# Two-layer hybrid blocks on one core: in blocks of 256 tokens, eight 512-column matmuls and then eight 256-column ones, in place of alternating pairs

## Chip, cores and metric

The kernel runs on one core of one Trainium2 chip. The time is device microseconds (us) of one execution on that core. Of the kernel before, three executions are timed; their median stands for it. A profile is of one execution.

## What is computed

The reference runs two transformer-like models, one behind the other, on a sequence of 256 tokens of width 1024 (16 meta tokens are set ahead of them for the first model). Each model has two layers, and each layer is a mixer and a squared-ReLU MLP, both added to a residual stream after an RMS norm. All data are fp32:

```python
def first_block(...):
    for layer in range(DEPTH):
        hn = rms_norm(h, g_mix[layer])
        if layer % 2 == 0:
            h = h + attention_mixer(hn, ...)
        else:
            h = h + short_conv_mixer(hn, w_in_conv[j], conv_w[j], w_out_conv[j])
        h = h + sq_relu_mlp(rms_norm(h, g_mlp[layer]), w_mlp_up[layer], w_mlp_down[layer])

def sq_relu_mlp(h, w_up, w_down):                  # w_up 1024 x 4096, w_down 4096 x 1024
    return jnp.square(jax.nn.relu(h @ w_up)) @ w_down
```

The second model has a differential attention and an mLSTM mixer, each again with an MLP of width 4096. So the order of the work is: attention (stage names a_...), MLP 0 (up0, dn0), convolution (c_in, c_out), MLP 1 (up1, dn1), differential attention (d_in, d_out), MLP 2 (up2, dn2), mLSTM (m_in, m_out), MLP 3 (up3, dn3). Up to the convolution the kernel carries 272 or 258 tokens, since the meta tokens and the convolution's halo are needed; from the last third of c_in on it carries the 256 tokens of the output only.

## The kernel before

Every weight matrix is cut into blocks of 1024 inputs by 128 outputs (one "feature block"). Weights come from HBM by DMA into four `raw` buffers of two blocks each. For each block, ScalarE writes the high part `whi` (rounded to the format that TensorE multiplies fast, fp32r) at line 545, and VectorE the remainder `wlo` = raw - whi at line 1113. Both sit in a ring of four buffers. Activations are kept as such a pair too: `x2`, `y2` and `hid2` hold for each slice of 128 inputs the high part of all tokens and then the low part. In the profile they are named x, y and hid.

A block's product is the sum over eight slices k of whi·xhi + whi·xlo + wlo·xhi. TensorE (the program `pe`) does it in one of two ways:

- `product` (lines 1973 to 1975): three matmuls a slice, each over all tokens (272, 258 or 256 columns), into the same PSUM columns.
- `paired` (lines 1979 and 1980), for 256 tokens: one matmul of 512 columns, whi against xhi and xlo side by side, fills both halves of a PSUM bank, and one matmul of 256 columns adds wlo·xhi to the second half. VectorE adds the halves when it reads the bank (line 1132).

`linear` (line 1998) does one block: `free_bank` waits until the bank has been read, then comes a wait for `w_lo` (both weight parts are there), the eight slices, and with the last matmul an increment of `w_used`, which gives the ring buffer back to ScalarE. Where `ready` is given (block 0 of a stage), TensorE also waits for each slice of the activations by itself. In `mlp` the up projection is a loop of four passes over eight blocks, through `linear`; block 0 of every pass has `ready`. The down projection is a loop of two passes over 16 blocks, and four consecutive blocks with the same output accumulate in one bank; `hid_ready` is waited for ahead of each. `d_out` and `m_out` call `paired` themselves, with blocks interleaved, and the second input projections `d_in` and `m_in` use `product`. MLP 3's down projection (`out_block`, lines 2558 to 2560) is laid out the other way round: activations are stationary, the weights stream through as 512 columns, three matmuls a slice, all of 512 columns.

Each engine's program is written out by hand, in order; engines are bound to each other by semaphores alone. Every matmul is preceded by its own load of 128x128 weights (LDWEIGHTS, PEld in the profile).

Of the kernel before, what the change touches and what calls it, by code (L numbers as in the profile page):

```python
# [12 lines left out]
KB = D // P  # L13
# [4 lines left out]
FB = FF // P  # L18
# [18 lines left out]
S = SEQ  # L37
# [9 lines left out]
RING = 4  # L47
# [97 lines left out]
def build(nc, d, out):  # L145
# [5 lines left out]
    for b, (_, g, _) in enumerate(blocks):  # L151
        last_block[g] = b
# [20 lines left out]
    with ExitStack() as ctx:  # L173
# [4 lines left out]
        def sb(name, shape, dt=F32, at=ctx):  # L178
            return at.enter_context(nc.sbuf_tensor(name, shape, dt))
# [4 lines left out]
        PS = ctx.enter_context(nc.psum_tensor("PS", [P, 8, 512], F32))  # L184

        raw = [sb(f"raw{i}", [P, 2 * D]) for i in range(RAW)]
        whi = [sb(f"whi{i}", [P, D], F32R) for i in range(RING)]
        wlo = [sb(f"wlo{i}", [P, D], F32R) for i in range(RING)]
# [17 lines left out]
        with ExitStack() as s:  # L206
            hid2 = sb("hid2", [P, FB * 2 * (T - HALO)], F32R, s)
            hh, hl = (hid2, 0), (hid2, 1)
# [60 lines left out]
        w_hi, w_lo, w_used, psum_read = Z["w_hi"], Z["w_lo"], Z["w_used"], Z["psum_read"]  # L269
# [4 lines left out]
        def std(ap):  # L274
            return ap.rearrange("p (k c) -> p k c", k=KB)
# [37 lines left out]
        def at(buf, n, tok):  # L313

            if isinstance(buf, tuple):
                return buf[0][:, bass.ds(n * (2 * T) + (buf[1] + tok[0]), tok[1])]
            return buf[:, bass.ds(n * T + tok[0], tok[1])]

        def hid(buf, n, count):
            return buf[0][:, bass.ds(n * (2 * count) + buf[1] * count, count)]  # L320

        def both(buf, k, tok):

            return buf[0].rearrange("p (k a t) -> p k a t", k=KB, a=2)[:, k, :, tok[0]:tok[0] + tok[1]]

        def both_hid(n, count):
            return hid2[:, n * 2 * count:(n + 1) * 2 * count].rearrange("p (a t) -> p a t", a=2)
# [33 lines left out]
        def bank(stage, o):  # L361

            if stage == "d_in":
                return D_T_BANK if o == 3 else o % 3
            return (O[stage] + o + 1) % PSR

        def a_bank(o):

            if o in (4, 5):
                return o + 2  # L370
            return (o + 1) % PSR if o < A_LEAD or o >= O["a_om"] else (o + 1) % 2
# [1595 lines left out]
        def _(pe):  # L1967
            mm = nc.tensor.matmul

            def product(b, k, cols, xs_hi, xs_lo, dst, first, last):  # L1970

                whi_b, wlo_b = cols(whi[b % RING], k), cols(wlo[b % RING], k)
                mm(dst, whi_b, xs_hi, start=first, stop=False)  # L1973
                mm(dst, whi_b, xs_lo, start=False, stop=False)  # L1974
                return mm(dst, wlo_b, xs_hi, start=False, stop=last)  # L1975

            def paired(b, k, xs_hi, xs_both, dst, first, last):

                mm(dst.rearrange("p (a t) -> p a t", a=2), std_cols(whi[b % RING], k), xs_both, start=first, stop=False)  # L1979
                return mm(dst[:, S:2 * S], std_cols(wlo[b % RING], k), xs_hi, start=False, stop=last)  # L1980

            def std_cols(buf, k):
                return std(buf[:, :])[:, k, :]

            def free_bank(stage, o, i=0):

                back = 3 if stage == "d_in" and o != 3 or stage == "d_out" and o < 3 else PSR
                if stage == "m_in" and o >= PSR:
                    j = o - PSR
                    if j in V_LAST or j + 1 in V_LAST:  # L1990
                        hd = (V_LAST.index(j) if j in V_LAST else V_LAST.index(j + 1))
                        pe.wait_ge(Z["m_vread"], TS * hd + 1 + (j in V_LAST))
                    else:
                        pe.wait_ge(psum_read, m_reads(j))
                elif O[stage] + o >= back:
                    pe.wait_ge(psum_read, i + (O[stage] + o - back + 1))

            def linear(stage, j, xhi, xlo, tok, ready=None, i=0, o=None, pair=False):


                b = B[stage] + j
                o = j if o is None else o
                free_bank(stage, o, i)
                pe.wait_ge(w_lo, i + (b + 1))
                order = [k for k, _ in ready[1]] if ready else range(KB)
                for n, k in enumerate(order):
                    if ready:
                        pe.wait_ge(ready[0], ready[1][n][1])
                    if pair:
                        last = paired(b, k, at(xhi, k, tok), both(xhi, k, tok), PS[:, bank(stage, o), :], n == 0, n == KB - 1)  # L2010
                    else:
                        last = product(b, k, std_cols, at(xhi, k, tok), at(xlo, k, tok), PS[:, bank(stage, o), 0:tok[1]],
                                       n == 0, n == KB - 1)
                last.then_inc(w_used, 1)

            def linear_first(stage, xhi, xlo, tok, ready, i=0, late=1):

                order = ready[1]
                for some in (order[:-late], order[-late:]):
                    for j in range(2):  # L2020
                        b = B[stage] + j
                        if some[0] is order[0]:
                            free_bank(stage, j, i)
                            pe.wait_ge(w_lo, i + (b + 1))
                        for k, count in some:
                            if j == 0:
                                pe.wait_ge(ready[0], count)
                            last = product(b, k, std_cols, at(xhi, k, tok), at(xlo, k, tok), PS[:, bank(stage, j), 0:tok[1]],
                                           k == order[0][0], k == order[-1][0])
                        if some[-1] is order[-1]:  # L2030
                            last.then_inc(w_used, 1)

            def x_blocks(n):

                return Z["x_ready"], [(k, 8 * n + k + 1) for k in range(KB)]
# [21 lines left out]
            def mlp(m, tok):  # L2057
                up, dn = f"up{m}", f"dn{m}"
                with pe.Fori(0, FB // 8) as i:
                    if m == 0:  # L2060
                        linear_first(up, xh, xl, tok, x_blocks(1), i * 8, 2)
                    for j in range(0 if m else 2, 8):
                        linear(up, j, xh, xl, tok, x_blocks(2 * m + 1) if j == 0 else None, i * 8, pair=m > 0)
                norm(2 * m + 1, tok[1])
                if m == 3:
                    return
                with pe.Fori(0, 2) as i:
                    for j in range(16):
                        ng, kc, n = j // 8, j % 8 // 2, j % 2
                        o, b = 2 * ng + n, B[dn] + j  # L2070
                        if kc == 0:
                            free_bank(dn, o, i * 4)
                        pe.wait_ge(w_lo, i * 16 + (b + 1))
                        pe.wait_ge(Z["hid_ready"], 2 + FB * m + KB * (kc + 1))
                        for k in range(KB):
                            kk = kc * KB + k
                            if m:
                                last = paired(b, k, hid(hh, kk, S), both_hid(kk, S), PS[:, bank(dn, o), :], kk == 0, kk == FB - 1)
                            else:
                                last = product(b, k, std_cols, hid(hh, kk, tok[1]), hid(hl, kk, tok[1]),  # L2080
                                               PS[:, bank(dn, o), 0:tok[1]], kk == 0, kk == FB - 1)
                        last.then_inc(w_used, 1)
# [3 lines left out]
            for _ in range(WARM):  # L2086
                last = mm(PS[:, 7, 0:2 * P], wlo[RING - 1][:, 0:P], wlo[RING - 1][:, 0:2 * P], start=True, stop=True)
# [140 lines left out]
            for some in (range(KB // 2), range(KB // 2, KB)):  # L2228
                for j in range(2):
                    pe.wait_ge(w_lo if some[0] else Z["w_first_lo"], j + 1)  # L2230
                    for k in some:
                        if j == 0:
                            pe.wait_ge(Z["x_ready"], k + 1)
                        last = product(B["a_in"] + j, k, std_cols, at(xh, k, FULL), at(xl, k, FULL), PS[:, a_bank(j), 0:T],
                                       k == 0, k == KB - 1)
# [16 lines left out]
            for n in range(N_A + 2):  # L2252
# [24 lines left out]
                m = n - 13  # L2277
# [239 lines left out]
            for j in range(2, M_BLOCKS):  # L2517
# [6 lines left out]
                if j == ROW_AT[0]:  # L2524
                    pe.wait_ge(Z["mg_rows"], 1)
                    pe.wait_ge(Z["m_rtok"], 1)
                    for a in range(TS):
                        last = nc.tensor.transpose(PS[:, MISC, a * ML_HEADS:(a + 1) * ML_HEADS], mgate[:, 5, a * P:(a + 1) * P],
                                                   ident[0:ML_HEADS, 0:ML_HEADS])
# [33 lines left out]
            for c in range(2):  # L2563
                whole = 16 if c == 0 else 16 - RING
                for j in range(whole):
                    for a in range(TS):
                        last = out_block(c, j, a)
                    last.then_inc(w_used, 1)
                    if c == 0 and j == 4:
                        pe.wait_ge(w_lo, B["dn3"] + RING + 1)  # L2570
                        pe.wait_ge(Z["norm_read"], 8)
                        for a in range(TS):
                            last = mm(PS[:, MISC, a:a + 1], rstd2[0:1, a * P:(a + 1) * P], ident[0:1, 0:1], start=True, stop=True)
                        last.then_inc(Z["out_rt"], 1)
            for a in range(TS):
                for j in range(16 - RING, 16):
                    last = out_block(1, j, a)
# [47 lines left out]
```

## Time and profile before

| | |
|---|---|
| median of 3 executions | 1220.39 us (1219.93 to 1220.52) |
| profiled execution, first to last instruction | 1219.5 us |
| TensorE busy | 1206.3 us, 99%, 8112 matmuls |
| VectorE busy | 900.6 us, 74% |
| ScalarE busy | 715.2 us, 59% |
| GpSimd busy | 251.7 us, 21% |
| HBM read | 206.69 MB, 172 GB/s over the span |

The profile gives no time for the profiled execution other than its span; the median of the timed ones lies 0.9 us above it. Busy times of TensorE count overlapping instructions once. A matmul's record runs from its start to its modelled end, some 150 ns past the start of the next one. So what a matmul costs is read from start to start (here called its step), not from the duration of its record.

### The profile page before, as it was taken

The numbers are of one execution on the slowest core, as the hardware profiler recorded it, in microseconds if no ns is written. First come the engines' busy times: TensorE is split into PE (matmuls) and PEld (weight loads), VectorE is DVE, ScalarE is ACT, GpSimd is POOL, SyncE is SP. The second block draws the span as 40 slices with busy tenths as digits, with TensorE's granted clock in tenths as the row PEclk, the third lists the DMA queues.
The fourth block names the chain that finished last, engine by engine and source line by source line (L and its number), as shares of the span: only waits on it lengthen the run. The fifth ranks groups of instructions, "written<-read, shape, count | busy, mean of one in ns | idle before, by whom it ended". The sixth has DMA issues, their size and how long they took to land.

```text
span 1219.5 us, 23664 instructions
## 1 busy us (share of the span) xinstructions
PE 1206.3 (99%) x8112; PEld 1105.9 (91%) x8112; DVE 900.6 (74%) x1554; ACT 715.2 (59%) x1306; POOL 251.7 (21%) x260
## 2 busy tenths in 40 slices
PE   8999999999999999999999999999999999999997
PEld 8998999999999988888899998888889998888886
DVE  5788877565557988775669868786667988877764
ACT  5657656564444556664447876665445787666343
POOL 4000024220010114430020003442102811444000
PEclk9999999999999999999999999999999999999999
DMA  9214236655557556555656427665555645665550
GB/s 295 93 44 152 79 108 205 186 191 175 178 194 231 174 173 207 183 195 174 199 182 203 140 86 212 185 190 189 173 173 174 207 139 149 215 194 183 186 193 35
DMA packets 194693, 208.79 MB, mean 171 GB/s; under 512 B 6103, under 2 KB 183352, under 8 KB 194488
## 3 DMA queue, kind: packets, MB, share of 16 engines
q1 hardware_dynamic: 192256, 202.78, 52.1%
q10 hardware_dynamic: 2360, 5.00, 1.3%
q8 instruction: 45, 0.74, 0.3%
q14 instruction: 32, 0.26, 0.1%
HBM read 206.69 MB, written 2.64 MB: 172 GB/s over the span
## 4 chain that ended last, share of the span: by engine, by line
PE 88%; DVE 5%; ACT 4%; issue 2%; DMA 0%; ACTq 0%; DVEq 0%
PE PS L1979 28%; PE PS L1980 14%; PE PS L1973 10%; PE PS L1974 10%; PE PS L1975 10%; PE PS L2558 2%; PE PS L2559 2%; PE PS L2560 2%; PE PS L2191 1%; PE PS L2213 1%; PE PS L2147 1%; DVE wlo L1113 1%; ACT whi L545 1%; PE PS L2322 1%; PE PS L2320 1%
## 5 line engine op out<-in xcount | busy, mean ns | idle before, releaser
L1113 DVE TENSOR_TENSOR wlo<-raw,whi 128x1024 fp32r<-128x1024 f32 x368 | 453.1, 1238 | 161.6 <-ACT whi L545 158.7
L545 ACT ACTIVATE whi<-raw 128x1024 fp32r<-128x1024 f32 x368 | 386.5, 1053 | 310.9 <-PE PS L1980 168.9
L1979 PE MATMUL PS<-x,whi 128*128 128x512 f32 x832 | 291.8, 395 | 0.2
L1980 PE MATMUL PS<-x,wlo 128*128 128x256 f32 x832 | 234.4, 282 | 0.0
L1973 PE MATMUL PS<-x,whi 128*128 128x258 f32 (+2 forms) x800 | 231.7, 290 | 0.8 <-issue 0.8
L1974 PE MATMUL PS<-x,whi 128*128 128x258 f32 (+2 forms) x800 | 229.0, 286 | 0.0
L1975 PE MATMUL PS<-x,wlo 128*128 128x258 f32 (+2 forms) x800 | 227.2, 284 | 0.0
L1979 PEld LDWEIGHTS PS<-x,whi 128*128 128x128 f32 x832 | 156.3, 188 | 36.5 <-DVE x L1090 1.2
L1882 POOL TENSOR_TENSOR act_s<-act_r 128x256 f32<-128x256 f32 (+1 forms) x128 | 143.5, 1121 | 211.0 <-ACT act_r L607 150.1
L1979 PE MATMUL PS<-hid,whi 128*128 128x512 f32 x512 | 179.0, 395 | 0.2
L1862 POOL TENSOR_TENSOR acc<-acc,sq 128x256 f32<-128x256 f32 (+2 forms) x64 | 54.0, 844 | 584.0 <-ACT sq L589 234.9
L1980 PEld LDWEIGHTS PS<-x,wlo 128*128 128x128 f32 x832 | 157.2, 189 | 0.0
L1973 PEld LDWEIGHTS PS<-x,whi 128*128 128x128 f32 x800 | 152.3, 190 | 2.7 <-issue 1.9
L1974 PEld LDWEIGHTS PS<-x,whi 128*128 128x128 f32 x800 | 151.3, 189 | 0.4
L1975 PEld LDWEIGHTS PS<-x,wlo 128*128 128x128 f32 x800 | 151.5, 189 | 0.0
L1980 PE MATMUL PS<-hid,wlo 128*128 128x256 f32 x512 | 142.6, 279 | 0.0
L1979 PEld LDWEIGHTS PS<-hid,whi 128*128 128x128 f32 x512 | 96.0, 187 | 23.1 <-DVE wlo L1113 0.8
L1132 DVE TENSOR_REDUCE tmp<-PS 128x256 f32<-128x512 f32 x120 | 82.8, 690 | 43.0 <-PE PS L1980 41.3
L1980 PEld LDWEIGHTS PS<-hid,wlo 128*128 128x128 f32 x512 | 96.4, 188 | 0.1
L1974 PE MATMUL PS<-hid,whi 128*128 128x258 f32 x256 | 72.6, 284 | 0.0
L1973 PE MATMUL PS<-hid,whi 128*128 128x258 f32 x256 | 72.4, 283 | 0.0
L1975 PE MATMUL PS<-hid,wlo 128*128 128x258 f32 x256 | 71.9, 281 | 0.0
(317 smaller groups left out, 2013.4 us busy)
## 6 DMA issues: line engine op xcount, KB each, us to landing
raw<-in_mlp_w SPq DMA_DIRECT2D x64, 1024.0 KB, 5.4
raw<-in_w_mlp_up SPq DMA_DIRECT2D x32, 1024.0 KB, 5.5
raw<-in_w_mlp_down SPq DMA_DIRECT2D x32, 1024.0 KB, 5.0
raw<-in_w_in_conv SPq DMA_DIRECT2D x12, 1024.0 KB, 5.0
raw<-in_attn_w_in SPq DMA_DIRECT2D x12, 1024.0 KB, 5.1
raw<-in_mlstm_w_in SPq DMA_DIRECT2D x12, 1024.0 KB, 5.8
raw<-in_w_in_attn SPq DMA_DIRECT2D x8, 1024.0 KB, 8.0
raw<-in_w_out_attn SPq DMA_DIRECT2D x4, 1024.0 KB, 5.0
```

The costliest lines, as they stand in the source:

```text
L545: A(part_view(whi, b), raw_view(b), ACT.Copy).then_inc(w_hi, 1)
L1113: V.tensor_tensor(part_view(wlo, b), raw_view(b), f32(part_view(whi, b)), ALU.subtract).then_inc(w_lo, 1)
L1132: return V.tensor_reduce(o, PS[:, bk, :].rearrange("p (a t) -> p t a", a=2), mybir.AxisListType.X, ALU.add)
L1862: Gp.tensor_tensor(acc[:, 0:count], acc[:, 0:count], sq[:, k % 2, 0:count], ALU.add).then_inc(Z["acc_ready"], 1)
L1882: Gp.tensor_tensor(act_s[:, j % 2, 0:count], act_r[:, j % 2, 0:count], act_r[:, j % 2, 0:count], ALU.mult)\
L1973: mm(dst, whi_b, xs_hi, start=first, stop=False)
L1974: mm(dst, whi_b, xs_lo, start=False, stop=False)
L1975: return mm(dst, wlo_b, xs_hi, start=False, stop=last)
L1979: mm(dst.rearrange("p (a t) -> p a t", a=2), std_cols(whi[b % RING], k), xs_both, start=first, stop=False)
L1980: return mm(dst[:, S:2 * S], std_cols(wlo[b % RING], k), xs_hi, start=False, stop=last)
L2558: mm(dst, x_h, w_h, start=k == 0, stop=False)
L2559: mm(dst, x_h, w_l, start=False, stop=False)
```

## The change

A new helper, `paired_block`, does a whole block: first the eight 512-column matmuls with `whi`, slice after slice, then the eight 256-column ones with `wlo`. `linear` uses it where `pair` holds and no `ready` is given, and `mlp` uses it in the down projections of MLP 1 and 2. Block 0 of every pass or stage that has `ready`, `d_out`, `m_out`, all of `product`, and `out_block` stay as they were. The number of matmuls, their sizes, their operands, the waits ahead of a block and the increment behind it are the same. In the new file the lines are 1985 (512 columns) and 1987 (256 columns).

```diff
+            def paired_block(b, xs_hi, xs_both, dst, first, last):
+
+                for k in range(KB):
+                    mm(dst.rearrange("p (a t) -> p a t", a=2), std_cols(whi[b % RING], k), xs_both(k), start=first and k == 0, stop=False)
+                for k in range(KB):
+                    done = mm(dst[:, S:2 * S], std_cols(wlo[b % RING], k), xs_hi(k), start=False, stop=last and k == KB - 1)
+                return done
+
...
                 free_bank(stage, o, i)
                 pe.wait_ge(w_lo, i + (b + 1))
+                if pair and not ready:
+                    last = paired_block(b, lambda k: at(xhi, k, tok), lambda k: both(xhi, k, tok), PS[:, bank(stage, o), :], True, True)
+                    last.then_inc(w_used, 1)
+                    return
...
                         pe.wait_ge(Z["hid_ready"], 2 + FB * m + KB * (kc + 1))
-                        for k in range(KB):
+                        if m:
+                            k0 = kc * KB
+                            last = paired_block(b, lambda k: hid(hh, k0 + k, S), lambda k: both_hid(k0 + k, S), PS[:, bank(dn, o), :],
+                                                kc == 0, kc == FB // KB - 1)
+                        for k in range(0 if m else KB):
                             kk = kc * KB + k
-                            if m:
-                                last = paired(b, k, hid(hh, kk, S), both_hid(kk, S), PS[:, bank(dn, o), :], kk == 0, kk == FB - 1)
-                            else:
+                            if not m:
```

On TensorE, where the last third of c_in begins (behind the last 258-column block), the order before reads as follows; the last two rows go on alternating until 16 matmuls are done:

```order
L1974 MATMUL PS<-x,whi 128x258
L1975 MATMUL PS<-x,wlo 128x258
L1979 MATMUL PS<-x,whi 128x512 [waits w_lo,psum_read]
L1980 MATMUL PS<-x,wlo 128x256
L1979 MATMUL PS<-x,whi 128x512
```

The same place in the changed kernel, the first two blocks of the 256-token part:

```order
L1974 MATMUL PS<-x,whi 128x258
L1975 MATMUL PS<-x,wlo 128x258
L1985 MATMUL PS<-x,whi 128x512 [waits w_lo,psum_read]
L1985 MATMUL PS<-x,whi 128x512 x7
L1987 MATMUL PS<-x,wlo 128x256 x8
L1985 MATMUL PS<-x,whi 128x512 [waits w_lo,psum_read]
```

Seven 256-column matmuls moved behind seven 512-column ones; the wait of a block is still with its first matmul. On TensorE at the start of a down projection (MLP 1), before:

```order
L2067 UNCONDITIONAL_BRANCH
L2067 ISA
L2073 ISA [waits psum_read]
L1979 MATMUL PS<-hid,whi 128x512 [waits hid_ready,w_lo]
L1980 MATMUL PS<-hid,wlo 128x256
L1979 MATMUL PS<-hid,whi 128x512
```

and in the changed kernel:

```order
L2079 UNCONDITIONAL_BRANCH
L2079 ISA
L2085 ISA [waits psum_read]
L1985 MATMUL PS<-hid,whi 128x512 [waits hid_ready,w_lo]
L1985 MATMUL PS<-hid,whi 128x512 x7
L1987 MATMUL PS<-hid,wlo 128x256 x8
```

The loop's branch and the waits stand where they stood. The programs of VectorE, ScalarE and SyncE are the same, instruction for instruction, and GpSimd's differs only in line numbers.

## Rows read from the trace of the kernel before

**Rows 1.** The page: busy time, TensorE's clock by slice (9 is full), the chain's shares.

```profile
PE 1206.3 (99%) x8112; PEld 1105.9 (91%) x8112; DVE 900.6 (74%) x1554; ACT 715.2 (59%) x1306; POOL 251.7 (21%) x260
...
PEclk9999999999999999999999999999999999999999
...
PE 88%; DVE 5%; ACT 4%; issue 2%; DMA 0%; ACTq 0%; DVEq 0%
```

**Rows 2.** What TensorE waited for: us in total, times, longest; the two longest.

```profile
PE PS L2147 <- ACT asq L696: 2.6, 1, 2.6
PE PS L2087 <- DVE wlo L1257: 1.5, 1, 1.5
```

**Rows 3.** Groups by form: busy us, mean ns of one record, idle us before.

```profile
L1979 PE MATMUL PS<-x,whi 128*128 128x512 f32 x832 | 291.8, 395 | 0.2
...
L1979 PE MATMUL PS<-hid,whi 128*128 128x512 f32 x512 | 179.0, 395 | 0.2
L1980 PE MATMUL PS<-hid,wlo 128*128 128x256 f32 x512 | 142.6, 279 | 0.0
...
L1979 PE MATMUL PS<-y,whi 128*128 128x512 f32 x192 | 68.6, 400 | 0.1
```

**Rows 4.** Timeline of TensorE in up1: start us, us of the record, then the instruction.

```profile
467.80 0.39 PE L1979 MATMUL PS<-x,whi 128*128 128x512 f32 x1
468.03 0.28 PE L1980 MATMUL PS<-x,wlo 128*128 128x256 f32 x1
468.15 0.40 PE L1979 MATMUL PS<-x,whi 128*128 128x512 f32 x1
...
473.40 0.39 PE L1979 MATMUL PS<-x,whi 128*128 128x512 f32 x1
```

**Rows 5.** Timeline in dn1, first pass (two rows) and second pass (two rows).

```profile
545.20 0.39 PE L1979 MATMUL PS<-hid,whi 128*128 128x512 f32 x1
...
587.84 0.40 PE L1979 MATMUL PS<-hid,whi 128*128 128x512 f32 x1
...
610.37 0.40 PE L1979 MATMUL PS<-hid,whi 128*128 128x512 f32 x1
...
615.66 0.40 PE L1979 MATMUL PS<-hid,whi 128*128 128x512 f32 x1
```

**Rows 6.** Timeline in dn3 (512 columns only): two stretches behind an interruption.

```profile
1125.34 0.39 PE L2559 MATMUL PS<-wlo,hid 128*128 128x512 f32 x1
...
1127.19 0.39 PE L2558 MATMUL PS<-whi,hid 128*128 128x512 f32 x1
...
1139.71 0.40 PE L2559 MATMUL PS<-wlo,hid 128*128 128x512 f32 x1
...
1141.55 0.39 PE L2558 MATMUL PS<-whi,hid 128*128 128x512 f32 x1
```

**Rows 7.** One line of dn3: records, ns min/median/max, first and last start us.

```profile
L2558 PE MATMUL PS<-whi,hid x96: 389/389/389, 1144.9 to 1209.5; 128*128 128x512 f32 x96
```

**Rows 8.** Timeline in m_in (256 columns only), two blocks.

```profile
939.20 0.28 PE L2456 MATMUL PS<-whi,x 128*128 128x256 f32 x1
...
943.86 0.28 PE L2457 MATMUL PS<-wlo,x 128*128 128x256 f32 x1
...
949.77 0.28 PE L1973 MATMUL PS<-x,whi 128*128 128x256 f32 x1
...
952.62 0.28 PE L1973 MATMUL PS<-x,whi 128*128 128x256 f32 x1
```

**Rows 9.** Timeline in d_in: six matmuls of 128 columns merged.

```profile
717.66 0.83 PE L2373 MATMUL PS<-d_pT,dvt 128*128 128x128 f32 x6
```

**Rows 10.** Stretch of up1: us, then busy us of each engine (instructions), clock, DMA.

```profile
455.00:540.00 85.00, 85.00 (x488) 74.62 (x487) 70.52 (x103) 55.01 (x92) 37.26 (x30) 1.00 0.60 187
```

## Prediction

> **What bounds the kernel now.** I read the page first: TensorE is busy 99% of the span, at the full clock (2.4 GHz) in every slice, and the chain that ended last lies on it for 88% [rows 1]. The view of its waits says the same from the other side: the two longest together are 4.1 us, both in the first attention, far from the change [rows 2]. In the groups by form the two lines that the change touches show 0.2 us of idle time [rows 3]. So a nanosecond taken out of each matmul there goes to the end, and what matters is the step, the time from one start to the next. The busy view can't give it, since records overlap; the timeline can.
>
> In up1, line 1979 starts at 467.80 us, line 1980 at 468.03 and 1979 again at 468.15; 16 pairs later it is 473.40 [rows 4]. So the 512-column matmul takes a step of about 231 ns, the 256-column one about 118 or 119, and a pair (473.40 - 467.80) / 16 = 350.0 ns. The columns alone need 512 / 2.4 + 256 / 2.4 = 320 ns at the granted clock, so 30 ns a pair are overhead. That overhead isn't one number. In the first pass of dn1, 123 pairs (16 blocks less five pairs) take 587.84 - 545.20 = 42.64 us, 346.7 ns each; in the second pass, 15 pairs take 615.66 - 610.37 = 5.29 us, 353 ns each [rows 5]. Same line, same operands, same clock, different loop pass: TensorE falls into a rhythm and stays in it, and rhythms differ by some 3 ns a pair.
>
> **What the change touches.** Blocks done by the new helper: 8 of c_in, 7 of c_out, 7 of 8 in each of 4 passes of up1, up2 and up3 (84), and 32 in each of dn1 and dn2 (64). That is 163 blocks, 1304 of the 1536 pairs that line 1979 shows [rows 3]. Before, I take 350.0 ns for the 99 blocks of x and y, 346.7 for three of the four down passes and 353 for the fourth (dn2's passes are both taken like dn1's first), which gives (99 x 350.0 + 48 x 346.7 + 16 x 353) / 163 = 349.3 ns a pair.
>
> **What is only moved.** Waits stay with the first matmul of a block and the increment of `w_used` with the last, so ScalarE, VectorE and SyncE see the same events, each earlier or later only by what TensorE gains or loses. Nothing is queued differently on their queues or on the DMA queues. A block takes 8 x 350 = 2.80 us. VectorE is busy 70.5 of 85.0 us in up1, ScalarE 55.0 [rows 10], so TensorE may take 1% less time there and their work still hides; VectorE would become the bound only if TensorE took 17% less. The blocks with per-slice waits keep the old order. All of this I cost at nothing.
>
> **The 512-column matmuls.** Seven of eight in a block are now followed by another of 512 columns, and no row shows that for x or hid as the moving operand. The nearest is dn3, where all are of 512 columns and the weights move. Settled, a triple there takes (1209.5 - 1144.9) / 95 = 680 ns, so the step is 226.7 ns [rows 7], some 4 ns less than in a pair. But it isn't so at once: behind an interruption eight steps take 1127.19 - 1125.34 = 1.85 us (231 ns each) in one place and 1141.55 - 1139.71 = 1.84 us (230 ns) in another [rows 6]. In the changed kernel a run is only eight long, and the 256-column run between two of them is a small interruption. The cost lies between 226.7 (settled) and 231 (never settles). I take 229, the middle.
>
> **The 256-column matmuls.** These now follow each other as in the `product` blocks of 256 tokens. There 40 steps take 943.86 - 939.20 = 4.66 us, 116.5 ns, in one place, and 24 steps take 952.62 - 949.77 = 2.85 us, 118.8 ns, in another [rows 8]. I take 118, close to what one has in a pair now. A load of weights must hide under one such step, where before every second load had a 512-column matmul to hide under. That looks like a new risk, but six matmuls of 128 columns, each with its own load, take 0.83 us with the last one's record in it [rows 9]; less that record (about 0.28) they step by 0.55 / 5 = 110 ns. A load thus needs at most 110 ns and fits under 118, as it does in the rows of m_in.
>
> **The sum.** A pair goes from 349.3 to 229 + 118 = 347.0 ns: -2.3 ns x 1304 = -3.0 us. The span goes from 1219.5 to 1216.5 us. The timed median lies 0.9 us above the span, so I predict 1217.4 us. The bounds of the two unknowns give 226.7 + 116.5 = 343.2 ns a pair (-8.0 us) and 231 + 118.8 = 349.8 ns (+0.7 us).
>
> A rule weighed against this. The rows show that the step is not the columns over the clock plus a constant: 230 to 231 and 226.7 ns for the same 512 columns [rows 4, 7]. The Trainium skill, in "TensorE: Matmul & The Clock Gate", section "Back-to-back issue gap", gives a warm gap of N / 2.4 + 2.5 ns, whoever the neighbour is. By it the sum would be zero, as the order doesn't enter, and its own size (215.8 ns) is under every step of 512 columns above. It is the second rival below.
>
> **The rivals.**
>
> 1. Full settling. The runs of 512 columns reach the settled step within a matmul or two. For it: dn3 holds 226.7 for 64 us on end [rows 7]. Against it: it took longer than that behind both interruptions [rows 6]. A pair at 226.7 + 116.5 to 118: -8.0 to -6.0 us, so about 1213.5 us.
>
> 2. No difference. The order doesn't matter: 231 ns belong to any 512-column matmul that has x or hid moving, and dn3 is quick because its operands are laid out differently. Then a pair stays at 349 to 350 ns, and the time is 1220.4 us, within 1 us. For it: both interrupted stretches show 231 and 230 [rows 6], which is the step of the pairs, and nothing in the trace shows a settled 512-column step with x moving. Against it: the interrupted stretches did settle in the end, with the same operands. (This is where the skill's formula leads; the trace disagrees with its size, and can't yet say about the order.) To this case belongs the one in which TensorE is faster but some stage's end hangs on another engine; rows 10 leave little room for that.
>
> 3. A worse rhythm: slower. The second pass of dn1 shows that the same instructions can lock into 353 ns a pair for a whole pass [rows 5]. The new order is a new rhythm of 16 matmuls, and it may lock into such a one in all stages. The price is 353 - 349.3 = 3.7 ns x 1304 = +4.8 us, so 1225.2 us. It decides the sign from 349.3 ns a pair on, and can be measured from 351.2 ns (2.44 us / 1304 = 1.9 ns above). For it: one of four down passes is in it. Against it: three of four are not, nor any of the up stages I looked at, and the runs of equal length in rows 6 to 8 all lie at or under the steps of the pairs.
>
> **How the numbers follow.** A measurement of this kernel can tell about 0.2%, 2.44 us, from no change. My forecast (some 347 ns a pair, 1215.5 to 1219.5 us) gets 0.43, full settling 0.12, no difference 0.32, the worse rhythm 0.13. A part of the forecast's case, 0.07, lies above 1217.95 and would count as the same. So faster is 0.36 + 0.12 = 0.48, the same 0.32 + 0.07 = 0.39, slower 0.13. The range leaves out about a third of full settling at the low end and half of the worse rhythm at the high end: 1213.4 to 1223.0 us.
>
> **What would show it.** In the timeline of up1 after, eight rows of line 1985 in a row: their steps should be above 226.7 at first and fall towards it, with a mean near 229; eight rows of line 1987 at 116 to 119. Block to block should be 8 x 347 = 2.776 us instead of 2.800. `d_out`, `m_out`, dn3 and the `product` blocks should keep their steps, and the waits of TensorE should stay where they are. The prediction is wrong in kind if the 512-column steps inside a run stay at 231 (second rival), if they exceed 234 or the 256-column ones exceed 120 (third), or if steps fall as forecast but a wait for `wlo` or for a bank grows on TensorE in the up stages.

## Result and the profile after

The change makes the kernel slower by about a quarter of a per cent. Nine executions of each give 1223.67 us after (1223.42 to 1224.37) and 1221.10 us before (1219.93 to 1221.35); the ratio is 1.0024, with a 95% interval of 1.0014 to 1.0033. The forecast was 1217.4 us with a range of 1213.4 to 1223.0. The time lies outside it, on the slow side, 1.5 us short of the third rival's 1225.2 us.

| | before | after |
|---|---|---|
| median of nine | 1221.10 us | 1223.67 us |
| profiled span | 1219.5 us | 1221.7 us |
| TensorE busy | 1206.3 us | 1207.8 us |
| a pair in up1 to up3, inside a pass | 350.0 ns | 354.2 ns in most blocks, 352.9 over a pass |
| a pair in dn1 | 346.7 ns, then 353.4 ns | 349.2 ns |
| a pair in dn2 | 346.7 ns | 349.2 ns |

First the page of the kernel after, for what did not move; it answers to [rows 1]:

```profile
PE 1207.8 (99%) x8112; PEld 1106.1 (91%) x8112; DVE 899.8 (74%) x1554; ACT 715.0 (59%) x1306; POOL 251.4 (21%) x260
...
PEclk9999999999999999999999999999999999999999
...
PE 89%; DVE 5%; ACT 4%; issue 2%; DMA 0%; ACTq 0%; DVEq 0%
```

TensorE is still busy 99% at the full clock, and the other engines do the same work. Its waits, with those of before in [rows 2] (lines are numbered anew):

```profile
PE PS L2161 <- ACT asq L696: 2.6, 1, 2.6
PE PS L1973 <- issue: 1.6, 1, 1.6
PE PS L2101 <- DVE wlo L1257: 1.5, 1, 1.5
```

The 1.6 us ahead of L1973 stand 9.7 us into the execution, far ahead of the change; the kernel before has 0.8 us at the same line. No wait came with the change, and the groups of the two new lines show none (us idle before them in the last column), as [rows 3] did:

```profile
L1985 PE MATMUL PS<-x,whi 128*128 128x512 f32 x736 | 188.4, 398 | 0.0
L1985 PE MATMUL PS<-hid,whi 128*128 128x512 f32 x512 | 128.8, 393 | 0.1
L1987 PE MATMUL PS<-x,wlo 128*128 128x256 f32 x736 | 102.0, 281 | 0.0
```

So the loss is in the steps themselves. The timeline of TensorE merges equal neighbours; one block of up1 and the start of the next read:

```profile
468.41 2.05 PE L1985 MATMUL PS<-x,whi 128*128 128x512 f32 x8
470.30 1.11 PE L1987 MATMUL PS<-x,wlo 128*128 128x256 f32 x8
471.25 0.40 PE L1985 MATMUL PS<-x,whi 128*128 128x512 f32 x1
```

Eight steps of 512 columns take 470.30 - 468.41 = 1.89 us, 236 ns each, and eight of 256 columns 0.95 us, 119 ns each. In the alternating order of up1 the 512-column steps are 231 and 234 ns by turns, 232.4 on average, and the 256-column ones 117.6. So the 512-column step is some 4 ns worse than before, and 10 ns worse than the settled step of [rows 7]. A block of dn1:

```profile
547.85 2.00 PE L1985 MATMUL PS<-hid,whi 128*128 128x512 f32 x8
549.69 1.11 PE L1987 MATMUL PS<-hid,wlo 128*128 128x256 f32 x8
550.64 0.40 PE L1985 MATMUL PS<-hid,whi 128*128 128x512 f32 x1
```

Here the 512-column steps are 1.84 / 8 = 230 ns, and the 256-column ones 119. Before, in the first pass of dn1, four rows in order are

```profile
545.20 0.39 PE L1979 MATMUL PS<-hid,whi 128*128 128x512 f32 x1
545.43 0.27 PE L1980 MATMUL PS<-hid,wlo 128*128 128x256 f32 x1
545.54 0.40 PE L1979 MATMUL PS<-hid,whi 128*128 128x512 f32 x1
545.78 0.28 PE L1980 MATMUL PS<-hid,wlo 128*128 128x256 f32 x1
```

and all pairs from 546 to 585 us have 231.5 and 115.1 ns on average. So with hid the long steps gained 1.4 ns and the short ones lost 3.9. Read one by one from the single starts in the trace, the run of dn1 is 233, 236, 228, 233, 230, 227, 227, 226 ns: it settles at 226.7 from the sixth on, as dn3 does. The run of up1 is 234, 236, 237, 237, 236, 237, 237, 236: it settles too, but at 236.7. The first new block of each pass, which follows an alternating block, doesn't settle (at 476.88 us: 231, 232, 229, 230, 233, 226, 236, 230). For up1 as a whole, I take 128 pairs, which reach over two passes:

```profile
476.88 0.39 PE L1985 MATMUL PS<-x,whi 128*128 128x512 f32 x1
...
522.05 0.39 PE L1985 MATMUL PS<-x,whi 128*128 128x512 f32 x1
```

A pair takes 45.17 us / 128 = 352.9 ns. In each pass there are six blocks of 354.2, the first new one with 348.2 and the alternating block 0 with 350.0.

**The sum of the profile.** Taken block by block from the starts in both traces, the 99 changed blocks of x and y (792 pairs) are 2.7 us longer, 3.4 ns a pair. Down projections: 400 pairs at 346.7 go to 349.2, +1.0 us, and the 112 that were at 353.4 gain 4.2 ns each, -0.5 us; block by block the trace has +0.4 us for all 512. Together +3.1 us. From the first 512-column matmul of c_in to the end, the execution after is 2.9 us longer. The spans (1221.73 and 1219.47 us) differ by 2.3 us only, because the work ahead of the change was 0.6 us shorter in this execution: c_in's first such matmul starts at 405.94 us after and at 406.56 us before. That start varies without the change too (406.01 us in a second profile of the kernel before).

One reading of [rows 5] has to be mended. The rhythm of 353.4 ns in dn1 doesn't begin with the second pass but in its third block, 591 us into the kernel, where two steps in a row take 353 and 337 ns instead of 118 and 232. Two such steps (398 and 336 ns) stand at the same block of dn2, and there the rhythm stayed at 346.7. The prediction's 123 pairs of [rows 5] reach five pairs into the second pass, still at 346.7.

### The profile page after: what moved, and what is told of

Same layout as the page of the kernel before. It is cut to its first block, busy times and chain, and to the rows that moved or that the text cites. A ratio compares the mean times of both kernels' runs of the same rounds, so it can differ in the third digit from the quotient of the medians.

```text
span 1221.7 us, 23664 instructions
## 1 busy us (share of the span) xinstructions
PE 1207.8 (99%) x8112; PEld 1106.1 (91%) x8112; DVE 899.8 (74%) x1554; ACT 715.0 (59%) x1306; POOL 251.4 (21%) x260
## 4 chain that ended last, share of the span: by engine, by line
PE 89%; DVE 5%; ACT 4%; issue 2%; DMA 0%; ACTq 0%; DVEq 0%
PE PS L1985 24%; PE PS L1987 12%; PE PS L1973 10%; PE PS L1974 10%; PE PS L1975 10%; PE PS L1979 4%; PE PS L2572 2%; PE PS L2573 2%; PE PS L2574 2%; PE PS L1980 2%; PE PS L2205 1%; PE PS L2227 1%; PE PS L2161 1%; DVE wlo L1113 1%; ACT whi L545 1%
## 5 line engine op out<-in xcount | busy, mean ns | idle before, releaser
L1973 PE MATMUL PS<-x,whi 128*128 128x258 f32 (+2 forms) x800 | 231.1, 289 | 1.6 <-issue 1.6
L1985 PE MATMUL PS<-x,whi 128*128 128x512 f32 x736 | 188.4, 398 | 0.0
L1985 PEld LDWEIGHTS PS<-x,whi 128*128 128x128 f32 x736 | 133.4, 190 | 25.5
L1973 PEld LDWEIGHTS PS<-x,whi 128*128 128x128 f32 x800 | 151.5, 189 | 3.5 <-issue 2.8
L1974 PEld LDWEIGHTS PS<-x,whi 128*128 128x128 f32 x800 | 151.1, 189 | 0.5
L1975 PEld LDWEIGHTS PS<-x,wlo 128*128 128x128 f32 x800 | 151.0, 189 | 0.0
L1985 PE MATMUL PS<-hid,whi 128*128 128x512 f32 x512 | 128.8, 393 | 0.1
L1985 PEld LDWEIGHTS PS<-hid,whi 128*128 128x128 f32 x512 | 92.2, 189 | 17.0 <-DVE wlo L1113 0.5
L1987 PEld LDWEIGHTS PS<-x,wlo 128*128 128x128 f32 x736 | 99.9, 189 | 8.5
L1987 PE MATMUL PS<-x,wlo 128*128 128x256 f32 x736 | 102.0, 281 | 0.0
L1987 PEld LDWEIGHTS PS<-hid,wlo 128*128 128x128 f32 x512 | 69.8, 190 | 5.0
L1973 PE MATMUL PS<-hid,whi 128*128 128x258 f32 x256 | 72.4, 283 | 0.0
L1987 PE MATMUL PS<-hid,wlo 128*128 128x256 f32 x512 | 71.4, 282 | 0.0
```

Of the source, the lines that this page charges most:

```text
L1987: done = mm(dst[:, S:2 * S], std_cols(wlo[b % RING], k), xs_hi(k), start=False, stop=last and k == KB - 1)
```

## Experiments

Three theories stood at the start. **A**: a run of 512-column matmuls settles at a slow step when the moving operand comes in two pieces (256 columns of the high part, then 16 unused columns, then 256 of the low part, as in x and y), and at a fast one when it is one piece (as in hid). **B**: it is the address at which x begins, or the distance of its slices. **C**: the rhythm is chance. The kernel before was timed again beside each group of runs, with medians from 1219.85 to 1221.56 us; a ratio below is to the kernel before of the same group.

### One piece instead of two, in both orders

In `both`, which describes the 512 columns of x and y:

```diff
-            return buf[0].rearrange("p (k a t) -> p k a t", k=KB, a=2)[:, k, :, tok[0]:tok[0] + tok[1]]
+            o = k * (2 * T) + tok[0]
+            return buf[0][:, o:o + 2 * tok[1]].rearrange("p (a t) -> p a t", a=2)
```

On the changed kernel:

> The changed kernel, but the 512-column matmuls of x and y read one unbroken piece of 512 columns (from the first of the 256 tokens on) instead of two pieces of 256 with 16 columns between; so their low-part product is formed of the wrong columns. Theory A (two pieces with a gap make the run of eight settle at 236.7 ns, one piece lets it settle at 226.7 ns as in the down projections): the runs in up1 to up3, c_in and c_out go to about 233, 236, 228, 233, 231, 227, 227, 227 ns, a pair from 353-354 to about 348 ns, the time from 1223.7 to about 1219.5 us. Theory B (it is where the rows of x begin, 64 bytes off a 128-byte line, or their distance of 2176 bytes): the runs stay at 236.7, the time at 1223.7 us.

Measured: 1220.68 us, 3.0 us under the changed kernel's 1223.67 (0.9994 of the kernel before, 0.9985 to 1.0003). Each against the kernel before of its own group, +2.57 and -0.88 us, it is 3.4 us, where theory A expected 4.2. In up1 the same 128 pairs:

```profile
476.72 0.40 PE L1986 MATMUL PS<-x,whi 128*128 128x512 f32 x1
...
521.32 0.40 PE L1986 MATMUL PS<-x,whi 128*128 128x512 f32 x1
```

That is 44.60 / 128 = 348.4 ns instead of 352.9, in up2 and up3 as well. Start address and slice distance were kept, so B falls as the cause of the 236.7 ns, and A holds in its amount a pair. Its picture of single steps doesn't: the runs of x now go 230, 233, 226, 236, 235, 227, 230, 233, a mean of 231, and never settle. One piece takes away the slow lock; at the old addresses it doesn't bring the fast one. On the kernel before:

> The kernel before with the same edit (one unbroken piece of 512 columns for x and y; the low-part product is of the wrong columns). Theory A: pairs of x and y go from 350.0 to the 346.7 ns of the down projections; 1024 pairs, -3.4 us: about 1217.7 us. Theory B: nothing moves, 1221.1 us.

Measured: 1223.84 us, slower than before by 1.0018 (1.0009 to 1.0027). All up stages stayed at 350.0 ns. The down projections, whose code and operands were as before, went to another rhythm in three of their four passes; in dn1

```profile
547.70 0.40 PE L1980 MATMUL PS<-hid,whi 128*128 128x512 f32 x1
...
590.10 0.40 PE L1980 MATMUL PS<-hid,whi 128*128 128x512 f32 x1
```

are 42.40 / 120 = 353.3 ns a pair, where the kernel before has 346.7. So in the alternating order two pieces cost nothing that one piece saves (A misses there), and a stage can change its rhythm though nothing in it was touched.

### Another layout, in both orders

For the 256-token stages x and y are laid out as hid is, high and low part of a slice side by side, with the same results; only c_in's x keeps its two pieces. In `at`, and likewise in `both` and where the mLSTM mixer writes y:

```diff
             if isinstance(buf, tuple):
+                if tok[0] >= N_META and len(tok) == 2:
+                    return buf[0][:, bass.ds(n * (2 * S) + ((S if buf[1] else 0) + tok[0] - N_META), tok[1])]
```

> The kernel before, with the same results: x and y are laid out for the 256-token stages as hid is, high part and low part of a slice side by side, 512 columns a slice (all but c_in, whose x keeps the old layout). Both theories A and B: pairs of x and y at 346.7 ns, some 960 pairs, -3.2 us: about 1217.9 us, faster than both kernels. If the rhythm depends on chance alone (theory C), it may be 346.7, 350 or 353 ns a stage.

> The changed kernel with the layout of the run before (high and low part of a slice side by side, but in c_in). Theories A and B: all stages behave as the down projections do after the change, 230 ns on average for the 512-column matmuls and 119-120 for the 256-column ones, 349.4 ns a pair: about 1221.2 us, slower than the kernel before with the same layout by 2.7 ns x 1304 = 3.5 us.

> The alternating kernel with the side-by-side layout, unchanged, profiled once more; its executions spread from 1220.6 to 1225.0 us. In the first profile up1 ran at 353.3 ns a pair, up2 and up3 at 346.8, with the same code. If an execution's chance decides which rhythm a stage takes, some stage changes place among 346.7, 350 and 353.3 now (up1 alone is worth 256 x 6.6 ns = 1.7 us). If code, layout and the stage's start decide it, the same values come again, as they did for the kernel before.

The alternating kernel with this layout took 1223.28 us, 1.0014 of before (1.0005 to 1.0023), with executions from 1220.58 to 1225.03 us. The order of the change with this layout took 1222.32 us, 1.0006 (0.9997 to 1.0015), from 1221.56 to 1223.22 us. So the order that loses in the old layout is no worse here: its median is 1 us lower, though the two intervals overlap. Its pairs are at 349.5 ns in the up stages and 349.2 in the down stages, as expected; the time was expected 1.1 us lower, and 3.5 us above the alternating kernel of this layout, which it isn't. A block of its up1:

```profile
485.56 2.00 PE L1989 MATMUL PS<-x,whi 128*128 128x512 f32 x8
487.40 1.11 PE L1991 MATMUL PS<-x,wlo 128*128 128x256 f32 x8
488.36 0.40 PE L1989 MATMUL PS<-x,whi 128*128 128x512 f32 x1
```

The single 512-column steps are 233, 236, 228, 233, 231, 226, 227, 227 ns, those of hid. So x does settle at 226.7 when it is laid out like hid, and what kept it from that in the run with one piece at the old addresses was where the slices begin or their distance (no run parts the two): theory B's quantity matters, but not for the loss. Settling gains nothing either: the 256-column steps behind it are 119 ns, and the pair (349.2) is no shorter than the unsettled 348.4.

The alternating ones were expected at 346.7 everywhere, and were not. The first profile has 353.4 ns in up1 and 346.7 in up2 and up3; up3 of this profile:

```profile
1061.26 0.39 PE L1983 MATMUL PS<-x,whi 128*128 128x512 f32 x1
...
1105.64 0.39 PE L1983 MATMUL PS<-x,whi 128*128 128x512 f32 x1
```

and of the second profile of the same kernel (one execution, 1224.48 us):

```profile
1062.93 0.40 PE L1983 MATMUL PS<-x,whi 128*128 128x512 f32 x1
...
1108.15 0.40 PE L1983 MATMUL PS<-x,whi 128*128 128x512 f32 x1
```

44.38 / 128 = 346.7 ns against 45.22 / 128 = 353.3 ns, same code, same data. The end of dn1 and the start of dn2 changed from 346.7 to 353.3 in the same way, up1 and up2 did not. This shows that with one-piece operands the alternating order has more than one rhythm and that an execution falls into one or the other. 128 pairs are worth 0.43 us for each 3.35 ns; several such changes could make up the spread of its executions, though only two executions were profiled.

### A gap put into the down projections

```diff
-            return hid2[:, n * 2 * count:(n + 1) * 2 * count].rearrange("p (a t) -> p a t", a=2)
+            o = n * 2 * count - (16 if n else 0)
+            return hid2[:, o:o + 2 * (count + 16)].rearrange("p (a t) -> p a t", a=2)[:, :, 0:count]
```

> The changed kernel, with the down projections' 512-column matmuls reading two pieces of 256 columns with 16 columns (64 bytes) between, as x has them (the pieces begin 64 bytes earlier; the product is formed of partly wrong columns). Theory A (two pieces settle at 236.7 ns): the runs of dn1 and dn2 go from 233, 236, 228, 233, 231, 227, 227, 227 to 233, then 237 throughout, a pair from 349.2 to about 353 ns, the time up by 512 x 4 ns = 2.0 us on the changed kernel, about 1225.7 us. Rival A2 (something else of x, not its pieces, keeps it at 236.7): dn1 and dn2 stay at 349.2 ns, 1223.7 us.

> As the run before, with a gap of 32 columns (128 bytes) between the two pieces. If the number of pieces matters (A), 353 ns a pair as well and 1225.7 us. If it is that the gap of 64 bytes puts the second piece on another half of a 128-byte line than the first, dn1 and dn2 stay at 349.2 ns and the time at 1223.7 us.

Measured, one execution each: 1226.08 us and 1225.51 us. From c_in on they are 1.6 and 1.3 us longer than the changed kernel, where A expected 2.0; the rest lies ahead of c_in. With the gap of 16 columns, the same block of dn1 as above:

```profile
548.88 2.02 PE L1986 MATMUL PS<-hid,whi 128*128 128x512 f32 x8
550.74 1.12 PE L1988 MATMUL PS<-hid,wlo 128*128 128x256 f32 x8
551.70 0.62 PE L1986 MATMUL PS<-hid,whi 128*128 128x512 f32 x2
```

The 512-column steps are 1.86 / 8 = 232.5 ns, the 256-column ones 0.96 / 8 = 120. Over 120 pairs that is 352.7 ns, and 351.8 with a gap of 32 (32 in place of 16 in the edit); without a gap 349.2. So a gap of either size costs 2.6 to 3.5 ns a pair in this order: the pieces count. (The edit also moves the first piece by as much as the gap is wide, and no run moves it alone.) Theory A's 353 is met, though the steps stay near 233 and don't lock at 236.7. That lock needs something more that x has and hid doesn't; no run shows what.

### Only the down projections changed

> Only dn1 and dn2 are done in runs of eight, c_in, c_out and the up projections alternate as before. In the profile before, dn1 had 346.7 and 353.4 ns a pair and dn2 346.7; runs of eight have 349.2. Theory A with theory R (in the alternating order the rhythm that a pass falls into, 346.7, 350 or 353.3 ns, is decided by how it starts; in runs of eight it is fixed): x stages at 350.0, dn stages at 349.2, time within 0.7 us of the kernel before, 1220.9 to 1221.9 us, and less spread between executions than before. If the down projections carried the loss: 1223 us or more.

In the changed kernel's `linear`:

```diff
-                if pair and not ready:
+                if False:
```

Measured: 1221.08 us (1220.89 to 1221.96), 1.0007 of before, 0.9998 to 1.0016. In the profile up1 to up3 are at 350.0 ns and dn1 and dn2 at 349.2 throughout. This is where A and the several rhythms put it: the down projections explain about 0.5 us of the loss (+1.0 and -0.5 in the sum above), the x and y stages the rest.

### Does the kernel before keep its rhythms?

> The kernel before, unchanged, profiled once more. Theory R: up and c stages at 350.0 ns a pair, but the four down passes need not repeat 346.7, 353.4, 346.7, 346.7; each may be at another of these values, 0.43 or 0.86 us apart a pass. Rival (code and layout alone decide the rhythm of each pass): the same four values again.

> The kernel before; TensorE's first wait of each pass of the down projections also waits for three semaphores that were reached long before. No matmul is moved. Theory R (a stage falls into its rhythm by the way it starts, to some nanoseconds): at least one of the four down passes leaves its rhythm (346.7, 353.4, 346.7, 346.7 ns a pair) for another of 346.7, 350, 353.3, worth 0.43 us a step and pass; the time lies between 1219.6 and 1223 us. Rival (operands and their addresses decide): all as before, 1220.5 us.

The edit of the second, in the loop of the down projections:

```diff
+                        if m and j == 0:
+                            pe.wait_ge(Z["const_set"], 5)
+                            pe.wait_ge(Z["warm"], 1)
+                            pe.wait_ge(Z["const_in"], 16)
```

Both missed what theory R expected. The second profile of the kernel before (1220.55 us) shows 350.0 ns in the up stages, 346.7 then 353.4 in dn1, and 346.7 in dn2, exactly as the first; the one with extra waits shows the same and takes 1219.89 us, 0.9998 of before (0.9988 to 1.0007). An additional wait of that kind disturbs nothing. So two-piece alternation had 350.0 ns in every profile of this study, and the several rhythms were seen with one-piece operands only. What picks one of them stays open.

And the changed kernel:

> The changed kernel once more, profiled. If runs of eight have one rhythm per layout, the up stages show 353 ns a pair and the down stages 349.2 in every stage again, within 0.2 ns.

1223.70 us; every stage repeats: 352.9 ns in the three up stages, 349.2 in the down stages. Its order has one rhythm for each layout.

### Shorter runs, and a version meant to beat both

In `paired_block`, groups of two slices (or four):

```diff
+                for g in range(0, KB, 2):
+                    for k in range(g, g + 2):
+                        mm(dst.rearrange("p (a t) -> p a t", a=2), std_cols(whi[b % RING], k), xs_both(k), start=first and k == 0, stop=False)
+                    for k in range(g, g + 2):
+                        done = mm(dst[:, S:2 * S], std_cols(wlo[b % RING], k), xs_hi(k), start=False, stop=last and k == KB - 1)
```

> Side-by-side layout, order in groups of two slices: two of 512 columns, two of 256. By theory S (a run of 512 columns starts at 233 and 236 ns and settles at 227 from the sixth on, whatever stands ahead) a pair takes (233 + 236) / 2 + 117 = 351.5 ns, worse than runs of eight (349.3): 1222.3 + 2.5 = 1224.8 us. If a short pattern can lock into a rhythm as the alternating one does, it may be 346.7 throughout: about 1219 us.

> Side-by-side layout, groups of four slices. Theory S: (233 + 236 + 228 + 233) / 4 + (114 + 119 + 120 + 120) / 4 = 232.5 + 118.3 = 350.8 ns a pair: 1222.3 + 1304 x 1.5 ns = 1224.3 us. If a short pattern locks, it may be 346.7 ns: about 1219 us.

> The changed kernel, with groups of two slices in place of eight, old layout (x and y in two pieces). c_in of the side-by-side kernel in groups of two, which kept two pieces, had 353.2 ns a pair. If two pieces cost once 512-column matmuls follow each other at all, up1 to up3, c_in and c_out show 353 ns and the down projections 348.4: about 1223 us. If the loss needs a run longer than two, they show 350 or less: about 1220.5 us.

Groups of four with the side-by-side layout: 1222.85 us, 1.0025 of before (1.0015 to 1.0034), 350.3 ns in up and 350.8 in down stages, as forecast from the first four steps of a run; the time was forecast 1.5 us higher. Groups of two missed the forecast to the good side: 1220.22 us, 1.0002 (0.9992 to 1.0012), at 348.1 ns in up and 348.3 in down stages. Its 512-column steps are 233 ns as expected, but the 256-column ones fall to 115.3 on average. In the old layout, with two pieces, groups of two take 1225.00 us (one execution); up1:

```profile
478.74 0.39 PE L1986 MATMUL PS<-x,whi 128*128 128x512 f32 x1
...
523.90 0.39 PE L1986 MATMUL PS<-x,whi 128*128 128x512 f32 x1
```

45.16 / 128 = 352.8 ns, all 512-column steps behind the first new block of a pass at 236 to 237 ns, even the one that is followed by a 256-column matmul. The time was expected at 1223 us; its excess lies ahead of the change, since c_in begins at 407.83 us here and from there on the execution is 0.4 us shorter than the changed kernel's 815.8. The loss a pair needs no long run.

But it doesn't come with every grouping. In the groups-of-four run, c_in still has x in two pieces; its seven later blocks, up to the first matmul of c_out:

```profile
408.81 1.10 PE L1990 MATMUL PS<-x,whi 128*128 128x512 f32 x4
...
428.36 0.39 PE L1983 MATMUL PS<-y,whi 128*128 128x512 f32 x1
```

19.55 / 56 = 349.1 ns a pair, less than the 350.8 that groups of four take with one piece. The same stage, in two pieces, has 354.2 ns in runs of eight and 353.4 in groups of two. Its 512-column steps go 237, 236, 230, 230 and 234, 226, 235, 230 ns by turns: the slow lock doesn't hold. So two pieces and 512-column matmuls in a row make the loss together in runs of eight and in groups of two, and not in groups of four. Why four differs is open, and the other stages were not run in groups of four with two pieces.

The last pair takes `paired_block` in groups of two, and in `at` and `both` the side-by-side layout for x alone (`both` isn't shown); c_in and c_out alternate:

```diff
+                if buf[0] is x2 and tok[0] >= N_META and len(tok) == 2:
+                    return buf[0][:, bass.ds(n * (2 * S) + ((S if buf[1] else 0) + tok[0] - N_META), tok[1])]
...
-                if pair and not ready:
+                if pair and not ready and stage[0] != "c":
```

> Same results as the kernel before. x alone is laid out side by side in the 256-token stages (not in c_in), y keeps its layout; up and down projections run in groups of two slices, c_in and c_out alternate as before. From the measured pairs (groups of two, one piece: 348.4 ns; up before: 350.0; down before: 346.7 to 353.4, mean 348.2): 672 up pairs x -1.6 ns = -1.1 us, down +0.1 us: 1.0 us under the kernel before of the same job, with a spread between executions under 1 us. If the layout brings the first block of each pass into a slow rhythm, as it did in d_out, the gain is gone.

> As the run before, but the down projections alternate. Up: -1.1 us. Down: each pass of 128 pairs falls into 346.7, 350 or 353.3 ns, so between -0.4 and +2.1 us against the kernel before, and executions differ by more than in the run before.

The first runs up and down projections in groups of two; up1:

```profile
476.51 0.40 PE L1990 MATMUL PS<-x,whi 128*128 128x512 f32 x1
...
521.08 0.40 PE L1990 MATMUL PS<-x,whi 128*128 128x512 f32 x1
```

44.57 / 128 = 348.2 ns. Its median is 1220.04 us (1219.72 to 1221.00) beside 1220.83 us of the kernel before in the same group; 0.9993, 0.9984 to 1.0002. The 0.8 us are near the 1.0 expected, but the interval includes no change, so it isn't shown to be faster than the kernel before; it does beat the changed kernel, whose ratio to before is 1.0014 to 1.0033. With the down projections alternating again it took 1222.37 us, 1.0013 (1.0004 to 1.0022): both down stages fell into 353.3 ns, though their code is that of the kernel before, where they mostly have 346.7. The larger spread that was expected didn't come (1.3 us in both). Groups of two in the down projections are thus worth 2.3 us in that kernel, and nothing in the kernel before, which has a better rhythm there.

## Why the prediction was wrong, point by point

- **What bounds the kernel**: right. TensorE is the bound before and after, no wait moved, and steps alone explain the difference (3.1 us by steps, 2.57 between the medians; the work ahead of c_in varies by some tenths of a us).
- **What is only moved, at no cost**: right. Idle time ahead of the two new lines is 0.1 us; VectorE and ScalarE do the same in the same stages.
- **The 512-column matmuls** ("I take 229, the middle"): this is the step that failed. Both bounds, 226.7 and 231 ns, came from dn3, where one piece of weights moves. For hid, also one piece, they held: 230 ns. For x and y the steps are 236.7 ns, outside the bounds, because their operand comes in two pieces; with one piece they are 231 ns. That is shown for this order by the run with one piece; why two pieces cost it is open. The prediction wrote that no row shows x moving in such a run, and then took the bounds of another operand as if they held for it. The upper end should have been open; the trace before already had 512-column steps of 232, 236 and 240 ns in the 353 ns rhythm of dn1. The 231 ns taken for the pairs of x is one of two steps that take turns, 231 and 234.
- **The 256-column matmuls** (118, "close to what one has in a pair now"): right for x (118 after, 117.6 before). For hid they take 119.1, only 1 ns more than taken, but they had been 115.1 in the pairs at 346.7. This is the whole loss of the down projections: +3.9 ns there against -1.4 in the 512-column steps. None is longer than 122 ns, so no load of weights shows as a wait; whether it adds to the 119 isn't shown.
- **The base of 349.3 ns a pair**: right on average, but one of its terms, 346.7 ns in the down passes, is one of several rhythms and no property of the stage's code alone (353.3 in the kernel with one piece for x, whose down projections are the same). A step taken from one profile of an alternating stage can be off by 6.7 ns a pair.
- **The sum**: -2.3 ns x 1304 was forecast, +3.1 us was found. 792 pairs of x and y lost 3.4 ns each instead of gaining 3, and 400 of the down pairs lost 2.5 where the prediction's own terms, 346.7 to 347.0, gave 0.3.
- **The rule**: the Trainium skill, in "TensorE: Matmul & The Clock Gate", section "Back-to-back issue gap", gives N / 2.4 + 2.5 ns for an isolated matmul; of a stream of weight loads and matmuls it says that both set the spacing. That neighbours don't enter was the prediction's reading. The steps here are 225 to 240 ns for 512 columns, where the formula has 215.8, and 112 to 124 ns for 256, at one clock: the formula is too small for this stream, and order and operand shape both enter.
- **The rivals**: the third had the right sign and, for x and y, the right price (353 ns a pair), and x's runs do lock into a slow rhythm. But it put that lock in all stages, for +4.8 us, and didn't name the operand as what decides it: hid's runs don't lock slowly, and the loss is half as large. Nor is it chance in the changed order: 352.9 and 349.2 ns repeat. What changes from one execution to the next was seen in the alternating order alone.

## What to carry to other kernels

Where TensorE never waits, read steps from start to start, separately for each kind of operand, before reordering matmuls: a step measured with a contiguous moving operand says nothing of one that comes in two pieces. If long matmuls are to follow each other, make their moving operand one contiguous piece first (here 353 to 348.4 ns a pair in runs of eight and in groups of two); if that can't be done, alternate long and short, or measure other group sizes, since four behaved otherwise than two and eight. And profile twice: a stage that runs in a rhythm can change it by 2% from one execution, or one distant edit, to the next, which is enough to hide or feign a gain of this size.

## What the runs showed of the hardware

- The cost of alternating 512- and 256-column fp32r matmuls, each with its own weights, comes in steps of about 3.3 ns a pair: 346.7, 350.0 or 353.3 ns, held for tens of us. With operands in two pieces it was 350.0 in all profiles; with one piece all three were seen, and two executions of one kernel differed in three stretches.
- Behind a run of 256-column matmuls, a run of 512-column ones takes five steps (233, 236, 228, 233, 230 ns) to reach its settled 226.7 ns with hid; so does x when laid out like hid. With x in two pieces it settles at 236.7 ns after one or two.
- A gap between the two halves of the moving operand costs, for a pair of 768 columns, 2.6 to 3.5 ns with hid (gap of 128 or 64 bytes, runs of eight) and 4.5 ns with x over a pass (64 bytes, runs of eight; 352.9 against 348.4). In groups of two it is about as much (352.8 against 348.1), and nothing could be seen of it when 512- and 256-column matmuls alternate. In groups of four it costs nothing: 349.1 ns in two pieces, 350.8 in one.
- Why the steps take these values, and what picks a rhythm, was not found.
